# Chunk attention: value units in two PSUM banks by turns, one reciprocal per score map

## The reference, cut to what matters

```python
q = rms_norm((hn @ w_q).reshape(bsz, s, N_HEADS, HEAD_DIM), q_norm_g)      # 16 heads of 64
def one_chunk(args):                                # 64 queries, 9 chunks of 64 keys
    ...
    sc = jnp.einsum("bqhd,bkhd->bhqk", qc, kc,
                    preferred_element_type=jnp.float32) * scale + bias
    valid = (start - left + jnp.arange(band)) >= 0
    sc = jnp.where(valid[None, None, None, :], sc, -1e30)
    p = jax.nn.softmax(sc, axis=-1).astype(vc.dtype)
    return jnp.einsum("bhqk,bkhd->bqhd", p, vc)
out = lax.map(one_chunk, (q_chunks, jnp.arange(n_chunks)))
return out.reshape(bsz, s, d) @ w_o
```

## Time and profile before

| | |
|---|---|
| time, median of 3 runs | 2496.67 us (2496.08 to 2497.7) |
| the profiled execution | 2501.48 us, its span 2499.7 us |
| mean granted TensorE clock | 0.996 |
| instructions | 32313 |
| busy: PE, PEld, DVE, ACT | 2475.2, 1968.4, 1482.8, 1126.3 us |

### The profile page before, as it was taken

The page is one execution under the profiler, slowest core; times in us unless marked ns, Lnnn a source line. Parts: engine busy times, 40 slices in busy tenths (PEclk is TensorE's granted clock), DMA queues, the critical chain, the costliest instruction groups (busy, mean ns, idle before and its releaser), DMA issues.

```text
span 2499.7 us, 32313 instructions
## 1 busy us (share of the span) xinstructions
PE 2475.2 (99%) x11940; PEld 1968.4 (79%) x11940; DVE 1482.8 (59%) x2486; ACT 1126.3 (45%) x2012; POOL 26.0 (1%) x18
## 2 busy tenths in 40 slices
PE   9999999999999999999999999999999999999999
PEld 7887888888776688888887877778877777777887
DVE  7987656566768753433456654664465665466445
ACT  6675433433545543432445544442354554444234
POOL 0000000000000000000000000000020000000002
PEclk9999999999999999999999999999999999999999
DMA  7623466666221122222231211212323121122233
GB/s 301 217 103 135 167 203 208 204 208 205 77 84 68 51 93 102 102 93 101 93 110 61 76 68 65 84 72 93 110 85 110 60 76 68 64 77 81 93 109 110
DMA packets 77901, 280.33 MB, mean 112 GB/s; under 512 B 8640, under 2 KB 8896, under 8 KB 77504
## 3 DMA queue, kind: packets, MB, share of 16 engines
q1 hardware_dynamic: 61056, 219.60, 24.6%
q10 hardware_dynamic: 16704, 58.79, 7.0%
HBM read 276.26 MB, written 2.10 MB: 111 GB/s over the span
## 4 chain that ended last, share of the span: by engine, by line
PE 91%; DVE 5%; ACT 2%; issue 1%; DMA 0%; ACTq 0%; SPq 0%; DVEq 0%
PE ps L222 26%; PE ps L224 25%; PE ps L223 25%; PE ps L1817 2%; PE ps L1914 2%; DVE wl L217 1%; PE ps L1887 1%; PE ps L1719 1%; PE ps L1821 1%; PE ps L1776 1%; ACT wh L214 1%; PE ps L506 1%; PE ps L512 1%; PE ps L1157 1%; PE ps L1992 1%
## 5 line engine op out<-in xcount | busy, mean ns | idle before, releaser
L217 DVE TENSOR_TENSOR wl<-raw,wh 128x1024 fp32r<-128x1024 f32 x372 | 456.8, 1228 | 591.9 <-ACT wh L214 591.9
L222 PE MATMUL ps<-xh,wl 128*128 128x512 f32 x1744 | 696.0, 399 | 8.3 <-ACT bC L1119 5.4
L224 PE MATMUL ps<-xh,wh 128*128 128x512 f32 x1744 | 680.7, 390 | 0.0
L223 PE MATMUL ps<-xl,wh 128*128 128x512 f32 x1744 | 680.4, 390 | 0.0
L214 ACT ACTIVATE wh<-raw 128x1024 fp32r<-128x1024 f32 x372 | 392.8, 1056 | 600.7 <-PE ps L224 589.7
L222 PE MATMUL ps<-bh,wl 128*128 128x512 f32 x1174 | 463.6, 395 | 3.4 <-DVE bl L1372 1.3
L224 PE MATMUL ps<-bh,wh 128*128 128x512 f32 x1174 | 457.2, 389 | 0.0
L223 PE MATMUL ps<-bl,wh 128*128 128x512 f32 x1174 | 457.1, 389 | 0.0
L222 PEld LDWEIGHTS ps<-xh,wl 128*128 128x128 f32 x1744 | 327.3, 188 | 127.2 <-issue 43.2
L224 PEld LDWEIGHTS ps<-xh,wh 128*128 128x128 f32 x1744 | 327.6, 188 | 70.1
L223 PEld LDWEIGHTS ps<-xl,wh 128*128 128x128 f32 x1744 | 327.7, 188 | 65.1 <-issue 1.2
(11 more groups left out here) (322 smaller groups left out, 2549.4 us busy)
## 6 DMA issues: line engine op xcount, KB each, us to landing
raw<-in_w SPq DMA_DIRECT2D x388, 512.0 KB, 3.2
bA<-in_ada ACTq DMA_DIRECT2D x74, 512.0 KB, 4.5
bC<-in_ada SPq DMA_DIRECT2D x9, 512.0 KB, 13.1
bD<-in_ada ACTq DMA_DIRECT2D x8, 512.0 KB, 4.4
bS<-in_attn_bias ACTq DMA_DIRECT2D x8, 512.0 KB, 3.1
bD<-in_ada SPq DMA_DIRECT2D x7, 512.0 KB, 14.9
bC<-in_ada ACTq DMA_DIRECT2D x6, 512.0 KB, 4.0
h<-in_x SPq DMA_DIRECT2D x4, 512.0 KB, 7.1
```

The costliest lines, as they stand in the source:

```text
L217: e.tensor_tensor(wl[p][:], raw[p][:], wh[p][:].bitcast(F32), ALU.subtract)\
L222: e.matmul(out, wl[p][:, blk, 0:M], xhi, start=start, stop=False)
L223: e.matmul(out, wh[p][:, blk, 0:M], xlo, start=False, stop=False)
L224: return e.matmul(out, wh[p][:, blk, 0:M], xhi, start=False, stop=stop)
```

## The change

The value unit of pair j is made in bank j % 2, and turned back into that same bank once ScalarE has copied it out. The other bank takes the blocks of the next pair meanwhile. The reciprocal of the row sums is taken for one map at a time, after that map's exponential, and the map is divided before the other map's sum is waited for. The second block's attention has functions of its own and is untouched.

```diff
--- before.py
+++ after.py
@@ -1174,15 +1174,14 @@
                         x = sc(n, m)[:, 0:steps[n]["nk"]]
                         done(e.activation(x, x, ACT.Exp, bias=nm(n, m), accum_out=rs(n, m)), f"{s}{n}ex{m}")
 
-                def scaled(n):
+                def scaled(n, m):
 
                     if dve:
-                        need(f"{s}{n}ex1")
-                        done(e.reciprocal(ri(n, 0, 2), rs(n, 0, 2)), f"{s}{n}ri")
-                        need(f"{s}{n}ri")
-                        for m in range(2):
-                            x = sc(n, m)[:, 0:steps[n]["nk"]]
-                            done(e.tensor_scalar(x, x, ri(n, m), None, ALU.mult), f"{s}{n}nr{m}")
+                        need(f"{s}{n}ex{m}")
+                        done(e.reciprocal(ri(n, m), rs(n, m)), f"{s}{n}ri{m}")
+                        need(f"{s}{n}ri{m}")
+                        x = sc(n, m)[:, 0:steps[n]["nk"]]
+                        done(e.tensor_scalar(x, x, ri(n, m), None, ALU.mult), f"{s}{n}nr{m}")
 
                 def turn(n):
                     if pe:
@@ -1346,18 +1345,19 @@
                     unit_read(u0 + j, 0, 0)
                     if j:
                         need(f"V{j - 1}tt")
-                copy_out(0, BK[0], raw_v)
+                copy_out(j % 2, BK[j % 2], raw_v)
                 if act:
                     split(u0 + j + 2, 0, 0)
-                BK[0] += 1
+                BK[j % 2] += 1
 
             def value_turn(j):
 
-                turn_tile(f"V{j}", 1, BK[1], lambda i: raw_v[:, P * i:P * i + P], lambda: e.wait_ge(s_bank[0], BK[0] + 1))
+                b = j % 2
+                turn_tile(f"V{j}", b, BK[b], lambda i: raw_v[:, P * i:P * i + P], lambda: None)
                 if dve:
                     need(f"V{j}tt")
-                    e.tensor_copy(v_tok(j), by_block(ps[1][:])).then_inc(s_bank[1], 1)
-                BK[1] += 1
+                    e.tensor_copy(v_tok(j), by_block(ps[b][:])).then_inc(s_bank[b], 1)
+                BK[b] += 1
 
             def out_high(j):
 
@@ -1414,8 +1414,8 @@
 
             for n in range(-1, N + 2):
                 j, i = n // NT, n % NT
-                if 0 <= n < N:
-                    scaled(n)
+                for m in range(2) if 0 <= n < N else ():
+                    scaled(n, m)
                 if n + 1 < N:
                     scores(n + 1)
                     if dve and i == NT - 1:
@@ -1431,7 +1431,7 @@
                         need(f"A{n - 1}st1")
                     bias_load(j + 1)
                 if 0 <= n < N and j < KD - 1:
-                    blocks(u0 + j + 1, 0, xh, xl, range(2 * i, 2 * i + 2))
+                    blocks(u0 + j + 1, (j + 1) % 2, xh, xl, range(2 * i, 2 * i + 2))
                 if 0 <= n < N and j == KD - 1:
                     pair_tiles(0, range(2 * i, min(2 * i + 2, KD - 1)))
                 if n + 1 < N:
@@ -1449,7 +1449,7 @@
                         value_out(j + 1)
                 if 0 <= n - 1 < N:
                     if pe and (n - 1) % NT == 0:
-                        e.wait_ge(s_bank[1], BK[1] + 1)
+                        e.wait_ge(s_bank[(n - 1) // NT % 2], BK[(n - 1) // NT % 2] + 1)
                     values(n - 1)
                 if i == 1 and 5 <= n < N:
                     out_high((n - 5) // NT)
```

## The result

The changed kernel takes 2491.48 us (median of 10 runs, 2488.19 to 2493.54) against 2497.59 us of the kernel before (10 runs): a ratio of 0.9971, interval 0.9963 to 0.9979, that is some 7.2 us less (5.2 to 9.2; the two medians lie 6.1 apart). Forecast were 7.4 us and 2489.3 us, with a range of 2487.0 to 2493.3.

A forecast was written before the change was run, and what follows sets the result against it. Chunk attention was taken as bound by engines waiting for one another, none full. Banks 3.5 us plus inverse 4.0 made 7.5, cut to 7.4 for small waits: 2496.67 to 2489.3 us, range 2487.0 to 2493.3.

The forecast's parts named there:

- TensorE's wait for the bank: Weight blocks waiting for the value copy out of PSUM: 0.91 us per boundary, VectorE passing 0.51; 3.5 us in all.
- The inverse per map: Second reciprocal in each of 32 steps, first scaling earlier in VectorE's gaps: net 4.0 us, 0.53 per period.
- 256 step: Head pair's step with 256 keys: no VectorE gap, so the added reciprocal costs 0.19 us, eight times, 1.5 us lost.
- The sum: Chunk attention's period: VectorE's cycle 16.10 - 0.51 - 0.53 = 15.06 us, longer than TensorE's floor of 14.80, so it rules.
- TensorE's floor: TensorE's need per head pair without its two waits: 16.10 - 0.91 - 0.39 = 14.80 us.
- The stage: Chunk attention, about 732 to 864 us: 3.5 + 4.0 = 7.5 us shorter, 7.4 after small new waits.
- small new waits: Waits such as TensorE's 512 transposes for ScalarE's 384-key copy, taking a little: 7.5 us becomes 7.4.
- The offset: Median of runs 4.81 us below the profiled execution, carried over: 2494.1 us profiled gives 2489.3.
- One part only: One edit pays, an unseen wait swallows the other: period 15.5 to 15.6 us, time 2492.7 to 2493.2; chance 0.16.
- TensorE alone: VectorE has more room than counted, TensorE's floor of 14.80 holds: 9.1 us less, 2487.6 us; chance 0.13.
- Hidden anyway: The waits are hidden, a shift on TensorE is eaten in the next step: 2496.7 us; chance 0.05.
- Slower by 32 reciprocals: VectorE alone bounds, first scaling misses the gaps: 32 steps pay 0.19 us each, 6.1 us, 2502.8 us; chance 0.04.

The follow-up runs named there:

- the two repeats: The changed kernel run again, unedited, against the kernel before: 2491.95 us (ratio 0.9970) and 2491.69 us (0.9966).
- the two halves: Changed kernel with only the two banks (inversion together as before): 2495.11 us; kernel before with only the inverse per map (old banks): 2494.07 us.
- the joint version: Changed kernel, but the 256-key step inverts both row sums together after the second exponential: 2489.61 and 2489.83 us.
- passes: Four extra TensorE passes of 128x512 between the stage's first two scores, added to the kernel with joint inversion in the 256-key step: 2487.18 and 2489.72 us.

## Why the prediction was right

**TensorE's wait for the bank** was taken for a gain of 0.91 us of which VectorE lets 0.51 through. Measured alone: 0.52. Right in mechanism and size. That the remainder would lengthen the wait before the 512 transposes was wrong: that wait stayed at 0.37, and the new one, 0.36, stands at the 128-key scores.

**The inverse per map** was summed by steps to 0.53 per period. Measured 0.52 on top of the two banks, with each step as counted; that it is 0.52 without them too is luck, as the loss in the 256 step is hidden there and another wait of nearly its size appears. The 256 step's loss of 0.19 was tested by its removal, 0.19, and the price of a reciprocal by an added one, 0.20 against the 0.19 to 0.20 of the earlier trace rows.

**The sum** had a cycle of VectorE of 15.06 us over a floor of 14.80. Measured 15.06 and 14.73. A hand count could come this close because all of the durations but one (the one-column reciprocal) were in the trace, the order of each queue is fixed by the program, and both limits were worked out, not only the one that moved. Had the change reached TensorE's floor, the count would have been 0.07 off.

**The stage** was to be 7.4 us shorter. The profiles that have the same low clock at its head show 132.26 - 124.25 = 8.0 and 7.8 us. Six of the seven intervals between value copies bring 1.04 us each, and the part behind the last copy 0.77, as counted (0.46 for the bank, 0.33 for three steps). The first interval brings 0.73 (15.53 to 14.80) where the sum has 0.53. The cause is in the traces: the 512 step of the first head pair has no L1372, so VectorE's gap was not 0.37 there but larger, and the first reciprocal and scaling fit into it as in the 384 step. The step gains 0.40 and not 0.19 (512-key to 128-key scores, 4.73 to 4.33 us); its row of the kernel before:

```profile
747.80 0.17 DVE L1181 RECIPROCAL crow<-crow 128x2 f32<-128x2 f32 x1 [0.88 <-ACT bA L1175]
```

The 0.1 us taken off for small new waits did not come either. The rest is the part up to the first value copy, to which the sum gives nothing: 6.81 us in the kernel before, 6.52 and 6.75 in the two repeats, 6.04 in the first profile of the changed kernel, which has no low clock there. It goes with the clock, and is no gain that the runs show.

**The offset** of profile and median, 4.81 us carried over unchanged, was the weak step. The profile's 2501.48 was an execution with much low clock, and the price of that was in neither sum nor range as a term of its own. The profiled execution after was one with nearly none: forecast 2494.1 us, measured 2488.19, now 3.3 under its median in place of 4.8 above. The median before rested on three runs; ten gave 2497.59 in place of 2496.67. So the forecast of 2489.3 lies 2.2 us under the measured median. The range held it because it was made wide for the rivals, not because the scatter of the clock was foreseen: that part is luck.

**The rivals.** One part only: falls with the two halves, which add. TensorE alone: falls, the period is 0.33 above the floor. Hidden anyway: falls. Slower by 32 reciprocals: falls, but its price per piece was right, and the joint version shows the one step in which it applied in the changed kernel.

## What to carry to other kernels

Where no engine is full, make a ledger for each engine of one period, with each gap named and the floor of the next engine beside it: a removed wait is worth only the distance to that engine's queue. Before an instruction is split in two so that its first half starts earlier, look for the gap that the half will stand in; where there is none, the split costs its fixed price (0.20 us here), so split in those steps alone. Two edits that shorten the same queue add up until the next floor, but check each step: a cost can be hidden as long as the other edit is missing, as the 256 step's reciprocal was with the old bank.

## What the runs showed of the hardware

The runs of one kernel scatter by nearly 6 us (the changed kernel from 2487.72 to 2493.54 over all its runs), and the scatter goes with TensorE's granted clock. Three stretches of the kernel before, one at the head of the stage and two behind it:

```profile
735.00:739.00 4.00, 4.00 (x14) 3.04 (x16) 3.01 (x9) 1.66 (x7) 0.00 (x0) 0.57 0.72 261
1400.00:1405.00 5.00, 5.00 (x31) 5.00 (x31) 1.47 (x3) 3.34 (x8) 0.00 (x0) 0.66 0.31 105
2022.00:2026.00 4.00, 4.00 (x13) 2.88 (x14) 1.27 (x5) 2.67 (x8) 0.00 (x0) 0.57 0.38 131
```

The same stretches of the profile after, where the code is the same but some 10 us earlier from 1400 on:

```profile
735.00:739.00 4.00, 4.00 (x22) 2.49 (x20) 3.85 (x11) 1.53 (x6) 0.00 (x0) 1.00 0.47 157
1390.00:1400.00 10.00, 9.98 (x58) 8.33 (x58) 6.66 (x13) 6.09 (x17) 0.00 (x0) 1.00 0.14 54
2008.00:2026.00 18.00, 17.98 (x103) 15.26 (x104) 11.25 (x20) 10.24 (x22) 0.00 (x0) 1.00 0.17 59
```

A stretch of low clock is some 3.4 us at half speed, 1.2 in place of 2.4 GHz (the second line lacks 0.34 of 5 us of full clock, so half of 3.4 us). Behind the stage one costs about 1.5 us: the spans from the stage's end were 1632.51 us with none (one profile), 1633.8 to 1634.2 with one (seven), 1635.3 to 1635.5 with two (four), and 1636.9 in the one profile that has one and a double one. They fall mostly at a few places (20 to 50, 735, 1400, 2020 us; in two profiles near 860), not every time: the profile after had TensorE's idle time of 1.17 us at 732 as the ten others without passes did, and alone of them no fall behind it. The idle time is thus not sufficient; in the two profiles where it was filled with passes no fall was seen there, which is too few to call it necessary. What decides between the two in a given execution stays open.
